# Two chained transformer blocks on one Trainium2 core: the squares of block 2's norms summed on TensorE, tile by tile, inside the residual phase

## What is computed

```python
def rmsnorm(x, g):
    xf = x.astype(jnp.float32)
    y = xf * lax.rsqrt(jnp.mean(xf * xf, axis=-1, keepdims=True) + RMS_EPS)
    return (y * g.astype(jnp.float32)).astype(x.dtype)

def hybrid_layer(x, ...):
    h = rmsnorm(x, norm_mix)
    ...                                   # projections, three attentions, gates -> merged
    x = x + merged @ w_out
    h = rmsnorm(x, norm_ffn)
    u = causal_depthwise_conv(h @ w_up, conv_w, conv_b)
    u_a, u_v = jnp.split(u, 2, axis=-1)
    return x + (jax.nn.silu(u_a) * u_v) @ w_down
...
for layer in range(2): x = hybrid_layer(x, ...)
return rmsnorm(x, norm_final)
```

## The kernel before

| phase | what it is | norm after it | tokens squared | units in the joint | matmuls per unit |
|---|---|---|---|---|---|
| 1 | last third of block 1's last feed-forward | "double": block 1's final one and norm_mix of layer 0 | 512 (squares of X and of X times final_g) | 2 | 18 |
| 2 | merged @ w_out, layer 0 | norm_ffn, layer 0 | 256 | 3 | 24 |
| 3 | last third of w_down, layer 0 | norm_mix, layer 1 | 256 | 2 | 18 |
| 4 | merged @ w_out, layer 1 | norm_ffn, layer 1 | 256 | 3 | 24 |
| 5 | last third of w_down, layer 1 | norm_final, the program's end | 256 | 2 | 18 |

## Time and profile before

### The profile page before, as it was taken

How to read it: one execution, slowest core, us unless ns; L and a number is a source line. 1 busy time by engine, 2 the same in 40 slices (tenths; PEclk the granted TensorE clock), 3 DMA queues, 4 the chain that set the end, 5 groups by cost and what they waited for, 6 DMA issues and landing times.

```text
span 2763.4 us, 44363 instructions
## 1 busy us (share of the span) xinstructions
PE 2659.9 (96%) x17192; PEld 2324.1 (84%) x17192; DVE 1463.4 (53%) x2113; ACT 1122.9 (41%) x1737; POOL 385.7 (14%) x374
## 2 busy tenths in 40 slices
PE   3999999999999999999999999989999999999998
PEld 2777879779787878777887799988999998899998
DVE  3333335565333335333346555576668777657776
ACT  2322224344222224222233454455556565565554
POOL 3100001033101011101020120120012012002211
PEclk8999999999999999999999999999999999999999
DMA  8555443214545445444323256544455654456563
GB/s 265 175 175 167 126 149 104 84 54 131 185 137 165 124 130 173 136 155 144 99 84 92 81 164 183 166 131 124 141 167 172 183 173 141 123 152 179 170 183 110
DMA packets 653900, 400.56 MB, mean 145 GB/s; under 512 B 11898, under 2 KB 614954, under 8 KB 653610
## 3 DMA queue, kind: packets, MB, share of 16 engines
q1 hardware_dynamic: 651914, 395.01, 47.2%
q0 software_dynamic: 1824, 3.29, 0.7%
HBM read 397.21 MB, written 1.05 MB: 144 GB/s over the span
## 4 chain that ended last, share of the span: by engine, by line
PE 86%; DVE 8%; ACT 3%; issue 1%; DMA 1%; POOL 0%; SPq 0%; DVEq 0%; ACTq 0%; POOLq 0%
PE psum L2173 17%; PE psum L2174 17%; PE psum L2175 17%; PE psum L2285 3%; PE psum L2287 3%; PE psum L2286 3%; DVE w_lo L1235 3%; PE psum L1952 2%; PE psum L2139 2%; PE psum L1990 2%; PE psum L2140 2%; PE psum L2141 2%; PE psum L1992 2%; PE psum L1991 2%; PE psum L2348 1%
## 5 line engine op out<-in xcount | busy, mean ns | idle before, releaser
L1235 DVE TENSOR_TENSOR w_lo<-raw,w_hi 128x1024 fp32r<-128x1024 f32 x609 | 785.8, 1290 | 673.1 <-ACT w_hi L894 671.4
L894 ACT ACTIVATE w_hi<-raw 128x1024 fp32r<-128x1024 f32 x609 | 638.7, 1053 | 417.1 <-PE psum L2175 268.1
L2173 PE MATMUL psum<-H_hi,w_hi 128*128 128x256 f32 (+1 forms) x2128 | 720.9, 339 | 13.3 <-DVE w_lo L1235 7.0
L2174 PE MATMUL psum<-H_hi,w_lo 128*128 128x256 f32 (+1 forms) x2128 | 714.9, 336 | 0.0
L2175 PE MATMUL psum<-H_lo,w_hi 128*128 128x256 f32 (+1 forms) x2128 | 714.4, 336 | 0.0
L2173 PEld LDWEIGHTS psum<-H_hi,w_hi 128*128 128x128 f32 x2128 | 404.9, 190 | 77.5 <-issue 28.9
L2175 PEld LDWEIGHTS psum<-H_lo,w_hi 128*128 128x128 f32 x2128 | 404.9, 190 | 41.8
L2174 PEld LDWEIGHTS psum<-H_hi,w_lo 128*128 128x128 f32 x2128 | 404.9, 190 | 38.9
L1840 POOL TENSOR_TENSOR G_lo<-g,G_hi 128x512 f32 (+3 forms) x132 | 141.9, 1075 | 1439.4 <-ACT G_hi L1010 1138.6
L2285 PE MATMUL psum<-H_hi,w_hi 128*128 128x256 f32 (+1 forms) x960 | 300.6, 313 | 2.4 <-ACT U L1132 2.4
L2287 PE MATMUL psum<-H_lo,w_hi 128*128 128x256 f32 (+1 forms) x960 | 285.4, 297 | 0.0
(11 more groups left out here) (246 smaller groups left out, 3954.9 us busy)
## 6 DMA issues: line engine op xcount, KB each, us to landing
raw<-ffn_w_in SPq DMA_DIRECT2D x176, 512.0 KB, 3.9
raw<-w_in SPq DMA_DIRECT2D x148, 512.0 KB, 3.9
quad_ring<-w_mod SPq DMA_DIRECT2D x66, 1024.0 KB, 6.7
raw<-w_up SPq DMA_DIRECT2D x88, 512.0 KB, 4.1
raw<-ffn_w_out SPq DMA_DIRECT2D x64, 512.0 KB, 3.7
raw<-w_out SPq DMA_DIRECT2D x32, 512.0 KB, 3.7
raw<-w_down SPq DMA_DIRECT2D x32, 512.0 KB, 3.8
raw<-ffn_w_out SPq DMA_DIRECT2D x32, 384.0 KB, 3.3
```

The lines of the kernel that those rows point to most:

```text
L894: act.activation(w_hi[:, slot, :], raw[:, slot, :], ACT.Copy).then_inc(hi_done, 1)
L1235: dve.tensor_tensor(w_lo[:, slot, :], raw[:, slot, :], w_hi[:, slot, :].bitcast(F32), ALU.subtract).then_inc(lo_done, 1)
L2173: pe.matmul(o, wh, xh[:, k, 0:width], start=k == 0, stop=False)
L2174: pe.matmul(o, wl, xh[:, k, 0:width], start=False, stop=False)
```

## The change

The squares of each tile are no longer added on POOL. Instead PE takes each tile's squares as the stationary operand and accumulates the partition sums in STAT over all eight tiles: tile_sums(nm, f). In the residual phase, ahead of unit u (u = 2 to 7), PE sums tile u-2. Tiles 6 and 7 are summed where pe_stats stood. Each group of sums first waits for the squares (sq_done), and ACT waits for tile_stat in place of sq_added before it reuses a buffer. In the phases 1, 3 and 5 unit 2 stands between the groups of tiles 0 and 1; in the phases 2 and 4, unit 2 is part of the joint, and both groups stand behind one another.

```diff
@@ norm(kind)
+        summed = kind in ("plain", "double", "final")
+        if summed:
+            nm["ts0"] = tile_stats[0]
+            tile_stats[0] += KD - 1
+            [ph for what, ph in plan if what == "gemm"][-1].more["summed"] = nm
-        sets["add"] += 9 if halves else KD - 2
+        sets["add"] += 9 if halves else 0 if summed else KD - 2
@@ ACT, square
-            if isinstance(k, int):
+            if "ts0" in norms[r]:
+                if k >= 2:
+                    act.wait_ge(tile_stat, norms[r]["ts0"] + k - 1)
+                else:
+                    act.wait_ge(stat_done, norms[r]["set0"])
+            elif isinstance(k, int):
@@ POOL, pool_gemm
+                if "summed" in ph.more:
+                    return
                 square_sum(ph.more["norm_next"], stat_width(nm) if nm else width)
@@ PE, pe_gemm, ahead of each unit
+                    if "summed" in ph.more and 4 * i + u >= 2:
+                        tile_sums(ph.more["summed"], 4 * i + u - 2)
@@ PE
+        def tile_sums(nm, f):
+            if f == 0:
+                pe.wait_ge(*spread_read[-1])
+            pe.wait_ge(sq_done, nm["sq0"] + f + 1)
+            n = stat_width(nm) // P
+            for tb in range(n):
+                ins = pe.matmul(STAT[:, tb:tb + 1], sq[:, f % 2, tb * P:tb * P + P], ones[:, 0:1], start=f == 0 and tb == 0,
+                                stop=f == KD - 1 and tb == n - 1)
+            ins.then_inc(stat_done if f == KD - 1 else tile_stat, 1)
+
         def pe_stats(nm):
             width = stat_width(nm)
+            if "ts0" in nm:
+                tile_sums(nm, KD - 2)
+                tile_sums(nm, KD - 1)
+                return
```

More of the change, by code:

```diff
@@ L304, in build_program @@
     sq_added = sem("sq_added")
+    tile_stat = sem("tile_stat")
     stat_done = sem("stat_done")
@@ L421, in build_program @@
     norms = []
+    tile_stats = [0]
     sets = dict(sq=0, add=0, set=0, root=0, half=0)
```

## The result

| | before | after |
|---|---|---|
| median | 2761.91 us (2761.11 to 2763.08) | 2790.13 us (2788.98 to 2792.18) |
| the profiled execution | 2765.37 us, span 2763.4 | 2789.95 us, span 2788.0 |

The ratio is 1.0103, with an interval of 1.0085 to 1.012. The prediction was 2781 us with a range of 2770 to 2790. Slower was right. The size was not: 9 us too low, just above the upper end. A second measurement of the same pair gave 1.0091 (1.0077 to 1.0105).

What follows compares the result with a forecast made beforehand. PE was taken as the bound, with DVE late in phases 1 and 3. Phase 1 -3.3, 2 and 4 +10.6, 3 +2.2, 5 +6.0, clock +4.7: +20.2 on 2765.4 is 2785.6, less 4.2 gives 2781 us; range 2770 to 2790.

Steps and rivals of the forecast that it cites:

- Waits: PE idles for the first squares: 2.4 us in phase 1, 2.8 in 3 and 5, 2.1 each in 2 and 4.
- the group: PE's price for one new group of sums: 0.53 us, in phase 1 0.90; 18.2 us over all phases.
- the clock behind the waits: Slow stretches of PE's clock behind the first waits of phases 1, 3 and 5, about 1.6 us each, 4.7 together.
- a slow stretch beyond some 4 us: A listed sign that the forecast is wrong: PE's clock staying low for longer than that.
- the base: Profiled execution 2765.4 us plus 20.2 gives 2785.6; 4.2 us taken off for the median of the runs shown: 2781.
- the credit of 6.0 us: Phase 1's end: 61 PE records in the slow stretch would take 7.0 us at full clock instead of 13.0.
- DVE is no longer late: Phase 1 without POOL's additions: DVE needs 1.9 us per unit against PE's 2.16; PE's end idle falls to 0.56 us.
- Cheap and warm: Rival: a group costs only its records, and no idle time lowers the clock; +10.7, 2772 us; chance 0.18.
- Long slow stretches: Rival: one-column sums keep PE's clock low, three phases lose 6.0 us instead of 1.6; +33, 2795 us; chance 0.10.
- The sums in the shadow: Rival: the sums' weight loads hide under the matmuls ahead, groups cost nothing; -2.7, 2758.5 us; chance 0.05.
- the early squares: Rival: ACT squares tile 0 earlier, so first waits and their clock cost vanish; +3.3, 2764.5 us; chance 0.05.

Runs made afterwards that it cites:

- 72 runs: The kernel before, unchanged, timed beside all the experiments: 2760.98 to 2768.76 us, median 2764.8 us.
- the waits alone: The kernel before with POOL's additions and its norm sums kept, only the changed kernel's first waits for squares put into PE's program: 2782.49 us, ratio 1.006.
- phase 3 alone: The change made in phase 3 only, the other phases as in the kernel before: 2770.51 us, ratio 1.0024.
- phase 5 alone: The change made in phase 5 only, the other phases as in the kernel before: 2772.65 us, ratio 1.0023.

## Why the prediction was right, and where it failed

**Right: the mechanism and its places.** All waits are where they were put, within 0.1 us but for the second one in phases 2 and 4 (1.07 in place of 1.4: with nothing behind it the first group takes 0.58 us to its end, where I had taken 0.37). Waits: 12.2 us predicted, 2.37 + 2 x 1.96 + 2 x 2.76 = 11.8 measured. PE becomes the last one everywhere, and DVE's relief is worth nothing beyond that. Later groups do not wait, and the idle ahead of the next phase is 0.56 to 0.62 us.

**Right with a small error: the group.** In the middle of phase 3 a group takes 0.37 us to the next start, and that matmul 0.20 us to its next in place of 0.12; in phase 1, with eight records, 0.81 and 0.20:

```profile
2284.55 0.28 PE L2191 MATMUL psum<-G_lo,w_hi 128*128 128x256 f32 x1
2284.66 0.50 PE L2227 MATMUL psum<-ones,sq 128*128 128x1 f32 x4
2285.03 0.36 PE L2189 MATMUL psum<-G_hi,w_hi 128*128 128x256 f32 x1
...
1798.08 0.95 PE L2227 MATMUL psum<-ones,sq 128*128 128x1 f32 x8
1798.89 0.36 PE L2189 MATMUL psum<-G_hi,w_hi 128*128 128x256 f32 x1
1799.09 0.28 PE L2190 MATMUL psum<-G_hi,w_lo 128*128 128x256 f32 x1
```

That is 0.45 and 0.89 us, where 0.53 and 0.90 were taken: 24 x 0.08 = 1.9 us too much. I had spread the pair's 0.16 us of change over one lone group; it is 0.08 per group.

**The step that failed: the clock behind the waits.** "I take it three times: 4.7 us." The windows have lost 10.2 us, so this term of the sum was less than half of what was measured. The prediction had named a slow stretch beyond some 4 us as a sign that it is wrong, and there are two. Behind the 2.76 us of phases 3 and 5 the stretch is not 3.6 us long, as behind 2.79 us in phase 3 before, but nearly twice that (the pieces at 0.50 are 6.8 us in each):

```profile
2276.80:2282.30 5.50, 5.50 (x26) 5.50 (x27) 2.89 (x6) 2.28 (x5) 0.00 (x0) 0.50 0.76 217
2753.76:2760.00 6.24, 6.24 (x29) 6.24 (x30) 2.51 (x5) 2.33 (x4) 0.00 (x0) 0.50 0.22 63
```

And phase 2, where I took no slow stretch because each piece of idle is short, has one behind its 0.89 and 1.07 us, while phase 4, with the same code and idle times, has none:

```profile
2070.11:2073.50 3.39, 3.39 (x19) 3.39 (x20) 2.88 (x4) 2.11 (x4) 0.00 (x0) 0.62 0.71 205
...
2550.01:2553.50 3.49, 3.49 (x30) 3.49 (x30) 2.89 (x4) 2.12 (x4) 0.00 (x0) 1.00 0.68 192
```

**The account of the two profiles.** 2789.95 - 2765.37 = +24.6 us, where +20.2 was predicted. Clock +5.5, waits -0.4, groups -1.9. One more slow stretch, about 1.6, lies behind the old idle of 2.55 us in phase 3's interval, which had full clock before. That is +4.8; some 0.7 us of the slow stretches lie in the waits themselves and cost nothing, and the rest is rounding.

**The other step that failed: the base.** "The median of the runs shown is 4.2 us lower, 2761.2, so 2781." The change's own sum on the profiled time gave 2785.6, within 5 us of the result; the two steps are about half of the 9 us each. The 4.2 us were subtracted as if they were a fixed overhead of profiling. They are not: the median of 72 runs is 2764.8, and the profiled 2765.37 was an ordinary execution. The changed kernel's profiled execution is 0.2 us from its median, and those of the other twelve runs lie from 2.8 us below to 2.7 us above theirs. The three runs shown were all at the low end, where 24 of the 72 lie. The 72 are three groups, each on a chip of its own, with medians of 2764.27, 2766.91 and 2763.36; whether chance or the chip put the three runs low is not shown. The same thing was in the sum from its other side: the credit of 6.0 us was a long slow stretch that the executions at 2761 to 2763 us most likely do not have, since it is worth 4.4 us by the intervals. Sum and base were taken from different executions. Which single runs had the long stretch was not seen, as only profiled ones show it.

**A reason that was wrong without a price.** "DVE is no longer late" once POOL is silent: without the sums it was late still, by 2.64 and 2.34 us, in phase 1 for ACT's sake. I had compared DVE's own period with PE's, and not ACT's, which feeds it. The sum survived because PE itself was later. Were PE less loaded, (2.64 - 0.56) + (2.34 - 0.56) = 3.9 us of idle and the clock behind it would have been missing.

**The rivals.** Cheap and warm fell twice: the waits alone brought slow stretches, and a group costs 0.08 us more than its records. Long slow stretches (2795) had too high a price: the stretches are longer than 3.6 us in phases 3 and 5, yet cost 3.4 to 3.5 us each and not 6. The measured time lies between the forecast and this rival. Its mechanism, the sums holding the clock down, stays open. The sums do not start a slow stretch: placed one unit later, without the waits, they had none behind them. They may lengthen one: behind the waits of phases 3 and 5 the pieces at 0.50 are 6.8 us in all six cases with the sums (both profiles of the changed kernel, phase 3 alone, phase 5 alone), and 3.4 us in both cases of the waits alone, of which this is phase 3:

```profile
2278.82:2282.24 3.42, 3.42 (x17) 3.42 (x17) 2.35 (x4) 1.80 (x4) 1.39 (x1) 0.50 0.77 221
2282.24:2290.00 7.76, 7.76 (x67) 7.76 (x66) 6.99 (x11) 6.19 (x10) 4.43 (x3) 1.00 0.73 212
```

But with the sums doubled they are 17.1, 3.4 and 10.2 us in phases 1, 3 and 5, so the number of sums does not settle it. The sums in the shadow and the early squares did not occur.

## What to carry to other kernels

When PE takes over work that depends on what it has just finished, place it behind one more unit: the same sums cost 21 us less so. Each of the 17 idle times of 2.3 to 2.8 us at these waits, in all profiles together, was paid for once more in clock. Give such work to PE only in the phases in which PE idles, and count the period of every engine in the feeding chain before promising that a relieved one will catch up. When a sum is made on a profiled execution, keep it there, and do not subtract a gap between it and a median of three runs unless something shows it to be an overhead.

## What was not expected of the hardware

The clock behind an idle time is not a function of that idle time alone. PE's idle of 2.55 us in front of G's products had full clock behind it in the first profile of before, and the low level in the second profile of the same kernel and in the changed one:

```profile
2099.83 0.45 PE L2173 MATMUL psum<-H_hi,w_hi 128*128 128x256 f32 x1 [2.56 <-DVE g L1431]
...
2099.90:2102.40 2.50, 2.50 (x12) 2.50 (x13) 2.34 (x4) 1.71 (x3) 1.48 (x2) 0.51 0.47 140
...
2109.00:2111.50 2.50, 2.50 (x12) 2.50 (x13) 2.34 (x4) 1.72 (x4) 1.46 (x2) 0.50 0.54 159
```

In all fourteen profiles the low level stands behind 14 of the 28 idle times of this kind, two in each. The same holds for 5.71 us (a slow stretch of 6.8 or 13.7 us in all) and for the pair of 0.89 and 1.07 us: low behind 5 of 8, in the changed kernel in phase 2 and not in phase 4, but in both where phases 2 and 4 alone were changed. There, phase 4:

```profile
2543.61:2547.00 3.39, 3.39 (x18) 3.39 (x18) 2.54 (x4) 1.76 (x3) 0.00 (x0) 0.50 0.79 221
```

What decides it was not found.

A one-column record costs 0.09 to 0.12 us wherever it stands: 0.37 / 4 in phase 3, 0.81 / 8 in phase 1, 2.3 / 20 where the sums were doubled. The Trainium skill (TensorE: Matmul & The Clock Gate, LDWEIGHTS) gives about 107 ns for a weight load of 128 columns; the trace lies around that, on both sides.
